# Gated one-hot rows made on VectorE per token, instead of compared on VectorE and gated on ScalarE

## The reference, cut to what matters

```python
def peer_ffn(h, w_query, sub_keys, expert_u, expert_v):
    ...
    cand_i = (si[:, :, 0, :, None] * N_KEYS + si[:, :, 1, None, :]).reshape(t, PEER_HEADS, PEER_TOPK * PEER_TOPK)
    top_s, pos = lax.top_k(cand_s, PEER_TOPK)
    idx = jnp.take_along_axis(cand_i, pos, axis=-1)
    gate = jax.nn.softmax(top_s, axis=-1).astype(h.dtype)
    ...
    def one_block(args):
        xi, ii, gi = args
        u = jnp.take(expert_u, ii, axis=0)
        a = jnp.einsum('ted,td->te', u, xi)
        w = gi * jax.nn.gelu(a, approximate=False)
        vv = jnp.take(expert_v, ii, axis=0)
        return jnp.einsum('te,ted->td', w, vv)
```

## Time and profile before

| | us |
|---|---|
| median of 3 runs | 1815.28 |
| lowest, highest | 1812.93, 1815.53 |
| profiled execution | 1814.15 |
| its span | 1812.4 |
| TensorE busy in the span | 1620.0 |
| VectorE busy | 1259.2 |
| ScalarE busy | 664.0 |
| GpSimd busy | 390.6 |

### The profile page before, as it was taken

How to read it: one execution, slowest core, us unless ns; L and a number is a source line. 1 busy time by engine, 2 the same in 40 slices (tenths; PEclk the granted TensorE clock), 3 DMA queues, 4 the chain that set the end, 5 groups by cost and what they waited for, 6 DMA issues and landing times.

```text
span 1812.4 us, 23042 instructions
## 1 busy us (share of the span) xinstructions
PE 1620.0 (89%) x7605; PEld 1306.1 (72%) x7605; DVE 1259.2 (69%) x2268; ACT 664.0 (37%) x1227; POOL 390.6 (22%) x326
## 2 busy tenths in 40 slices
PE   1999988999889999999999999688888888989996
PEld 0454565545489889989999999666666676768784
DVE  6457255339977889988888888666666666766556
ACT  2111133212378269438633333132323222323333
POOL 1103200000010003002366666422222222220000
PEclk9889999999989999999999999889999899999998
DMA  9853500000266459647999999988889787887663
GB/s 357 291 187 141 209 1 1 0 0 20 74 204 227 146 178 324 242 150 264 326 412 413 413 413 412 396 281 275 282 294 327 260 268 276 305 281 237 196 213 111
DMA packets 172763, 426.15 MB, mean 235 GB/s; under 512 B 13068, under 2 KB 62220, under 8 KB 169496
## 3 DMA queue, kind: packets, MB, share of 16 engines
q1 hardware_dynamic: 135808, 291.06, 45.3%
q0 software_dynamic: 36864, 134.23, 20.5%
q10 hardware_dynamic: 24, 0.02, 0.0%
HBM read 372.84 MB, written 52.43 MB: 235 GB/s over the span
## 4 chain that ended last, share of the span: by engine, by line
PE 55%; DVE 18%; DMA 13%; SPq 5%; issue 4%; ACT 4%; POOL 1%; DVEq 0%; ACTq 0%; POOLq 0%
PE bank L1153 7%; DMA shared<-gelu_dense 7%; PE bank L1154 7%; PE bank L1157 7%; PE bank L1097 5%; SPq L479 5%; PE bank L1099 5%; PE bank L1098 5%; PE bank L951 5%; PE bank L1026 3%; PE bank L961 3%; PE bank L1112 3%; DMA hT<-in_expert_u,idx_slot 2%; ACT weights L794 2%; DVE u_lo L1486 2%
## 5 line engine op out<-in xcount | busy, mean ns | idle before, releaser
L1153 PE MATMUL bank<-v_hi,w_hi 128*128 128x512 f32 x768 | 310.2, 404 | 81.9 <-DVE w_lo L1587 81.7
L1097 PE MATMUL bank<-h_hi,u_hi 128*128 128x384 f32 x1024 | 348.9, 341 | 23.0 <-DVE u_lo L1486 23.0
L1098 PE MATMUL bank<-h_lo,u_hi 128*128 128x384 f32 x1024 | 345.0, 337 | 0.0
L1099 PE MATMUL bank<-h_hi,u_lo 128*128 128x384 f32 x1024 | 345.0, 337 | 0.0
L1154 PE MATMUL bank<-v_lo,w_hi 128*128 128x512 f32 x768 | 306.6, 399 | 0.0
L867 ACT ACTIVATE v_hi<-weights 128x1024 fp32r<-128x1024 f32 x128 | 135.5, 1059 | 302.7 <-PE bank L1157 249.0
L1157 PE MATMUL bank<-v_hi,w_lo 128*128 128x512 f32 x768 | 242.0, 397 | 0.0
L1153 PEld LDWEIGHTS bank<-v_hi,w_hi 128*128 128x128 f32 x768 | 149.3, 194 | 123.3 <-DVE v_lo L1583 70.0
L1097 PEld LDWEIGHTS bank<-h_hi,u_hi 128*128 128x128 f32 x1024 | 194.4, 190 | 27.3 <-DVE u_lo L1486 16.6
L1583 DVE TENSOR_TENSOR v_lo<-weights,v_hi 128x1024 fp32r<-128x1024 f32 x128 | 156.5, 1222 | 77.3 <-ACT v_hi L867 75.0
L1486 DVE TENSOR_TENSOR u_lo<-weights,u_hi 128x1024 fp32r<-128x1024 f32 x128 | 156.0, 1223 | 66.8 <-PE bank L1099 65.7
(11 more groups left out here) (233 smaller groups left out, 2195.9 us busy)
## 6 DMA issues: line engine op xcount, KB each, us to landing
weights<-in_uT SPq DMA_DIRECT2D x128, 512.0 KB
weights<-in_expert_v SPq DMA_DIRECT2D x128, 512.0 KB, 4.8
weights<-in_w_ada SPq DMA_DIRECT2D x12, 2048.0 KB, 9.6
gates_dense<-weights SPq DMA_DIRECT2D x24, 1024.0 KB, 6.4
shared<-gelu_dense SPq DMA_DIRECT2D x64, 384.0 KB
weights<-gates_dense SPq DMA_DIRECT2D x16, 1536.0 KB, 13.4
gelu_dense<-weights SPq DMA_DIRECT2D x32, 384.0 KB
gelu_dense<-final_row SPq DMA_DIRECT2D x32, 384.0 KB
```

Source lines behind the costliest of these rows:

```text
L1097: nc.tensor.matmul(a, uh[:, k, :], h2_hi[:, :, k, :], start=(k == 0), stop=False)
L1098: nc.tensor.matmul(a, uh[:, k, :], h2_lo[:, :, k, :], start=False, stop=False)
L1099: ins = nc.tensor.matmul(a, ul[:, k, :], h2_hi[:, :, k, :], start=False, stop=(k == KC - 1))
L1153: nc.tensor.matmul(acc, wh, v_hi[:, r % 2, cols], start=begin, stop=False)
```

## The change

hot_i is made with its gate in one step on VectorE: for each of the 8 tokens of a half one instruction over 128 columns compares the row 0..127 with the token's key i and multiplies by the token's gate, key and gate both being per partition scalars. hot_j is made as before. ScalarE's gate_rows is gone with its semaphore hot_gated; what waited for it waits for hot_made.

```diff
-            def gate_rows(half):
-                act.wait_ge(hot_made, half + 1)
-                for q in range(HTOK):
-                    token = half % (P // HTOK) * HTOK + q
-                    rows = hot_i[:, half % HALVES, q, :]
-                    ins = nc.scalar.activation(rows, rows, ACT.Copy, scale=turned[:, half * HTOK // P % 2, 2, token:token + 1])
-                ins.then_inc(hot_gated, 1)
-
...
                 if d >= 2:
-                    act.wait_ge(hot_gated, (d - 1) * P // HTOK)
+                    act.wait_ge(hot_made, (d - 1) * P // HTOK)
...
-                gate_rows(d * P // HTOK)
                 product(m)
                 m += 1
-                gate_rows(d * P // HTOK + 1)
...
-                    if c < CHUNKS - 1:
-                        gate_rows(2 * g + 2)
-                        gate_rows(2 * g + 3)
...
             def build(half):
-                pe.wait_ge(hot_gated, half + 1)
+                pe.wait_ge(hot_made, half + 1)
...
                 at = half % (P // HTOK) * HTOK
-                for which, rows in ((1, hot_j), (0, hot_i)):
-                    key = turned[:, half * HTOK // P % 2, which, at:at + HTOK]
-                    ins = tt(rows[:, half % HALVES], iota128.unsqueeze(1).broadcast_to([P, HTOK, P]),
-                             key.unsqueeze(2).broadcast_to([P, HTOK, P]), ALU.is_equal)
+                picked = turned[:, half * HTOK // P % 2]
+                tt(hot_j[:, half % HALVES], iota128.unsqueeze(1).broadcast_to([P, HTOK, P]),
+                   picked[:, 1, at:at + HTOK].unsqueeze(2).broadcast_to([P, HTOK, P]), ALU.is_equal)
+                for q in range(HTOK):
+                    ins = ts(hot_i[:, half % HALVES, q, :], iota128, picked[:, 0, at + q:at + q + 1], picked[:, 2, at + q:at + q + 1],
+                             ALU.is_equal, ALU.mult)
                 ins.then_inc(hot_made, 1)
```

More of the change, by code:

```diff
@@ L331, in program @@
         gates_ready, iota_made = sem("gates_ready"), sem("iota_made")
-        hot_made, hot_gated, built = sem("hot_made"), sem("hot_gated"), sem("built")
+        hot_made, built = sem("hot_made"), sem("built")
         build_read = sem("build_read")
```

## The result

The changed kernel took **1824.42 us** in the median (1822.64 to 1826.73, eight runs), where the kernel before took 1815.4 beside it (1811.03 to 1821.07, eight runs). The ratio is 1.0048 [1.0031, 1.0066], or +8.8 us [5.6, 12.0]: slower by half a per cent, clear of the noise, inside the forecast range and 2.6 us under the forecast of 1827. The profiled execution took 1824.94 with a span of 1823.2. That is 10.8 more than before, of which the rows cannot give all to the change, as the last part of the account says.

The account below looks back on a forecast made before the run. TensorE's 7.95 us chunk was the floor, VectorE close behind at 7.97 and becoming the bound of d = 1 and 2. 9.4 + 2.5 = +11.9 us, from 1815.28 to 1827; range 1811 to 1845.

Parts of the forecast that it names:

- Step 1: Gatings removed from ScalarE, builds wait for VectorE directly; whole gain bounded by TensorE's idle time, 2 × 5.3 = 10.6 us.
- Step 2: hot_j's table kept on VectorE: comparisons of 1024 columns follow every 1.137 us, 0.070 of it for each instruction.
- Step 3: Eight 128-column instructions added per half on VectorE: p = 0.247 us each, double column rate and two scalar fetches paid.
- Step 4: VectorE's chunk becomes 9.65 us, passing TensorE's 7.95 and bounding d = 1 and 2: +4.7 per stage, +9.4 for two.
- my formula: VectorE's chunk 5.70 + 16p; stage change is 7 × (chunk − 7.95) − 1.9, against 5.3 us of lag before.
- my 0.20: Turning point between gain and loss at p = 0.20 us per new VectorE instruction; below it the change wins.
- Step 5: d = 0 has no dots: VectorE's chunk needs 7.4 us, under 7.95, so TensorE covers it: zero.
- Step 6: Ahead of the chunks a longer first half table delays u_lo by 0.83 us without slack: three stages, +2.5.
- Step 7: After the last chunk, 3.5 us of VectorE's lead over the next tile's selection is lost but covered: zero, 1.2 as bound.
- Step 8: No DMA or SP and GpSimd queue work moved; TensorE bounds after the last stage, so a shift is carried to the end.
- Rival D: GpSimd's gather issues hold up VectorE's new instructions in d = 1 and 2: 28 us more, 1855; chance 0.04 in full.
- The chances: Forecast case 0.46, A 0.12, B 0.19, C 0.12, D 0.04, near even 0.07; outcomes faster 0.23, within 0.17, slower 0.60.

Follow-up runs that it names:

- no scalar: Changed kernel with both per partition scalars of the hot_i instruction replaced by immediates (real keys and gates left out): 1800.68 us, ratio 0.9917 to the kernel before.
- one scalar: Changed kernel with the key as per partition scalar and an immediate in place of the gate: 1809.48 us, ratio 0.997 to the kernel before.
- half the columns: Changed kernel with hot_i's instructions over 64 of the 128 columns, the rest of the table left as it was: 1820.59 us, ratio 1.0021 to the kernel before.
- scalar-tensor-tensor: Changed kernel with hot_i made per token with the key as scalar and the gate as a broadcast tensor: 1831.73 us, ratio 1.0085 to the kernel before.
- mix of 2: In d = 1 and 2, two tokens per half by the new instruction, six compared together and gated by ScalarE; d = 0 as before: 1813.88 us, ratio 0.9989.
- mix of 2 in bf16: Two new, six compared tokens per half in all stages, compared in bf16 with tokens innermost, u_lo queued before the tables: 1809.59 us, ratio 0.9976 to the kernel before.
- uneven halves: The bf16 mix with first half 2 new and 6 compared tokens, second half 4 and 4, in all stages: 1803.97 us, ratio 0.994 to the kernel before.
- d = 0 alone: The change made in stage d = 0 only, d = 1 and 2 as in the kernel before: 1815.38 us, ratio 1.0.
- u_lo first: Changed kernel with u_lo queued ahead of the first two half tables: 1821.2 us, ratio 1.0047; again on another chip 1826.74, ratio 1.006, to the kernel before.
- second chip: Another chip, where the unaltered changed kernel was run again: 1828.82 us, ratio 1.0075 to the kernel before.
- d = 1 and 2 alone: The change made in stages d = 1 and 2 only, d = 0 as in the kernel before: 1823.89 us, ratio 1.0053.

## Why the prediction was right, step by step

One row holds all the kernels together: the stage of d = 1 and what it gives when it counts twice, for d = 1 and 2 (66.15 is the kernel before).

```
kernel               VectorE p   chunk   stage d=1   2 x (stage - 66.15)   measured [95%]
no scalar            0.134       7.98    59.45       -13.4                 -15.1 [-19, -11]
one scalar           0.196       8.88    64.58        -3.1                  -5.4 [-8.9, -2.0]
half the columns     0.224       9.26    67.34        +2.4                  +3.8 [-0.2, +8.0]
changed              0.257       9.81    71.10        +9.9                  +8.8 [+5.6, +12.0]
scalar-tensor-tensor 0.262       9.93    72.05       +11.8                 +15.4 [+11, +19]
mix of 2             -           8.71    65.50        -1.3                  -2.0 [-4.2, +0.2]
mix of 2 in bf16     -           8.51    64.13        -4.0                  -4.4 [-7.1, -1.6]
uneven halves        -           8.21    61.70        -8.9                 -10.9 [-15, -7]
```

Every measured interval holds the figure of its stages. What happens there is nearly the whole effect. (The chunk is the mean of seven, from u_lo to u_lo; in the kernel before it is 8.67, since the 8.77 of the earlier trace rows alternate as 7.97 and 9.58.)

- **Step 1, the whole gain is bounded by the idle time, 10.6: wrong in size.** With VectorE out of the way the stages fall from 66.15 to 59.45 and from 66.19 to 59.47, 6.7 us each, not 5.3, and the kernel without scalars gained 15. The 5.3 are what the rows leave idle; but the rows count more busy time for the same work while it has to wait. Here is the stage of d = 1, the kernel before and then the kernel without scalars:

```profile
667.65:733.80 66.15, 60.88 (x426) 58.40 (x426) 61.35 (x78) 59.66 (x162) 23.97 (x17) 1.00 0.87 308
```

```profile
664.98:724.44 59.46, 59.46 (x426) 58.61 (x426) 59.01 (x165) 26.57 (x47) 15.06 (x15) 1.00 0.92 332
```

  The same 426 matmuls are 60.88 us busy in one and 59.46 in the other: 5.3 of idle time and 1.4 of this make the 6.7.
- **Step 2** (70 ns for each instruction, 1.137 for 1024 columns): L1459 takes 1.13 to 1.14 from start to start.
- **Step 3, p = 0.247: right in each part.** 0.137 without scalars was 0.134; the double rate was 0.033 us for 64 columns; two scalars were 0.123 where I took 0.110. Together that is 0.010 more, and with it 0.16 us per chunk. The Trainium skill, VectorE: DVE Perf Modes, section "The perf-mode tier table", gives the double rate to tensor_scalar in fp32; the 0.033 us agree.
- **Step 4, +4.7 per stage: 4.95 and 4.90 measured, by errors that nearly cancel.** The chunk was 9.81, not 9.65. By my formula that is 7 × (9.81 − 7.95) − 1.9 − 5.3 = 5.8. Against the stage that TensorE alone sets, 59.45, the lags are 11.65 (changed), 12.6 (scalar-tensor-tensor), 7.9 (half the columns) and 5.1 (one scalar). 7 × (chunk − 7.95) less 1.4 gives 11.6, 12.5, 7.8 and 5.1. So the credit at the end of the stage is 1.4, a number fitted to these four kernels, and not 1.9, and what it is set against is the old lag of 6.7 and not the 5.3 of the idle rows. The longer chunk is worth +1.1, the smaller credit +0.5, the larger old lag −1.4. That is why the kernel with one scalar surprised me: it is 7 × 0.93 − 1.4 − 6.7 = −1.6 per stage, where −1.9 − 5.3 gave −0.7. The old lag of 6.7 is 7 × (8.67 − 7.95) = 5.0 from the chunks and 1.7 at the end of the stage, where the last two builds still wait 0.40 us for the gating and 0.86 for the copy. The stages alone part into gain and loss at a chunk of 7.95 + 8.1 / 7 = 9.11, p = 0.213, where my formula has 0.205; with the tables ahead, which my 0.20 counts, it is about 0.21.
- **Step 5, d = 0 covered: right.** TensorE is busy for all of it, the stage is 59.30 instead of 59.58, and the kernel with d = 0 alone came out at 1.0 [0.9985, 1.0014].
- **Step 6, +0.83 in each of three stages: right.** From the turned rows to the first chunk's u_lo it is 9.17 us in all three stages before (510.48 to 519.65 in the first) and 10.05, 10.07 and 10.07 after: +0.9. In d = 0 the shorter stage gives 0.3 back, and 0.6 stay. In d = 1 and 2 all of it stays. What my expectation for u_lo first had wrong is that another order of the queue gives it back: of the 0.9 it wins 0.4 there.
- **Step 7, a lead of 3.5 lost and covered: right, or too careful.** From the first chunk's u_lo to the last one's, seven chunks, d = 1 grows by 8.0 us (68.68 for 60.66). From there to the turned rows of d = 2 it was 86.67 before and is 83.66 after: 3.0 come back, since that u_lo was early before and is late now, and a last build ends 4.95 later, not 8.0. That makes the step's cost zero: from turn to turn it is 162.39 for 156.50, +5.9, which is the 0.9 ahead and the 4.95 of the stage. In the changed kernel on the second chip, and with d = 1 and 2 alone, it is 82.10 and +4.3, 1.6 in favour. This is the clock again. The rows behind the stage, up to the turned rows, of the changed kernel in its first profile and on the second chip:

```profile
738.00:819.00 81.00, 76.76 (x431) 75.65 (x430) 71.30 (x255) 27.38 (x37) 2.29 (x3) 0.98 0.53 183
...
778.60:782.00 3.40, 3.40 (x12) 3.40 (x12) 2.73 (x13) 0.00 (x0) 0.00 (x0) 0.50 0.81 275
```

```profile
736.00:817.00 81.00, 76.77 (x441) 75.65 (x440) 72.28 (x257) 28.50 (x40) 2.29 (x3) 1.00 0.54 185
```

  In the first the granted clock is 0.50 (1.2 GHz for 2.4) from 778.6 for 3.4 us, in which TensorE does 12 matmuls; in the 20 us before, at 1.00, it was busy for 17.44. In the second it stays at 1.00. All fourteen traces part this way: with such a stretch it is 81.3 to 81.5 us from the end of the stage to the turned rows, without one (five traces) 79.9 to 80.0. The five are all kernels in which VectorE is the bound, but three others of that kind have the stretch, so whether the change itself makes it rarer stays open.
- **Step 8, carried to the end: right.** From the rows it is −0.1 for d = 0, +4.3 to +5.9 for d = 1, 0.9 + 4.9 = +5.8 for d = 2: +10.0 to +11.6 us. With the same stretches of low clock on both sides it is +0.6, +5.9 and +5.8, which is 12.3, where the sum had 11.9. That d = 0 looks like zero and d = 1 sometimes like +4.3 goes with the clock, which the forecast did not look at. The medians say +8.8 [5.6, 12.0], and +13.6 [9, 18] on the second chip. The profiled pair's own +10.8 is no better witness: the turned rows of d = 0 come at 507.96 after and at 510.48 before, 2.5 us earlier with nothing changed ahead of them, and 1.7 us are added behind the stages.
- **Rival D did not occur in the changed kernel.** In d = 0 GpSimd issues nothing and eight new instructions take 2.13 us; beside the two gathers of each chunk they take 2.13. A small form of it shows in other kernels. Without scalars, the eight beside the gathers take 1.27 us and the next eight 1.16:

```profile
686.03 1.27 DVE L1462 TENSOR_SCALAR weights<-ada 128x128 f32<-128x128 f32 x8
```

```profile
686.09 0.98 POOL L611 DMA_INDIRECT hT<-in_expert_u,idx_slot  x1 [0.30 <-issue]
```

  One instruction is longer there, 0.25 us for 0.135, once per chunk, and it is the one during which the second gather's issue ends. With one scalar the first of the eight takes 0.04 longer, which is why that chunk is 8.88 and not 5.70 + 16 × 0.196 = 8.84. What lay behind the 0.68 of the earlier trace rows no run tested.
- **The chances.** Those of the cases add up to 0.62 for slower and 0.15 for within, where the prediction has 0.60 and 0.17; nothing hangs on it.

The right answer came by the right mechanism. The term that was most mis-sized is the room, 5.3 for 6.7. The errors of step 4 cancelled by luck, and near the turning point they would have mattered.

## What to carry to other kernels

Count per partition scalars as work: here each cost 0.061 us per instruction, nearly as much as the 128 columns themselves (0.067 at two columns a cycle), so taking a multiply off ScalarE and putting it on an engine that was already at the floor, by way of 8 small instructions, lost more than it saved. Before moving work, compare each engine's chunk with the floor of the stage (7.95 against 7.97 here), and take the room from a run with the suspect taken away, since idle time read from the rows was a fifth too small. When two engines are both near the floor, share the work so that the loop between them is shortest: what won was fewer and cheaper gatings in the loop, with a table that VectorE could still make in time. And before a microsecond in a trace is put down to a change, compare TensorE's granted clock over the same stretch.

## What the runs showed of the hardware

- **Scalars add up.** 128 columns of compare and multiply take 0.134, 0.196 and 0.257 us from start to start with none, one and two of them.
- **The new instructions make GpSimd's issue shorter.** The second gather of a chunk took 1.98 us before, when two comparisons of 1024 columns lay beside it. After it is

```profile
680.67 0.94 POOL L611 DMA_INDIRECT shared<-in_expert_u,idx_slot  x1 [0.30 <-issue]
```

  beside the tensor-scalars that begin at 680.61. It is 0.97 without scalars, 1.97 where d = 1 is as before, 1.71 in the first mix (768 columns of comparison) and 1.31 with the comparison in bf16. The Trainium skill, SBUF — State Buffer, section "Who interferes with whom", says that "A DVE instruction with two SBUF inputs contends with a GpSimd instruction that reads SBUF"; these rows agree. It also says that VectorE in a two-port mode and GpSimd block each other fully; with the new instructions, at two columns a cycle, no row shows either engine held for a whole instruction of the other. What shows is at most 0.12 us on one VectorE instruction per chunk. Issues are not on the path here, and no run isolated the cause.
- **A bf16 comparison with all operands adjacent** went at two columns a cycle: 0.47 us from start to start for 768 columns. ScalarE paid for the layout: from start to start a gating of 128 columns takes 0.36 us when it reads every sixth bf16 element and 0.31 when it reads every fourth (both in the kernel with uneven halves). Reading adjacent fp32 elements it was 0.29.
- **TensorE's clock moves the stretches between the stages.** One stretch of 3.4 us at a granted clock of 0.50 went with 1.6 and 1.4 us more from the end of the stage of d = 1 to the next turned rows, in two pairs of traces of one and the same kernel: 81.49 against 79.92 in the changed kernel, 81.34 against 79.90 with u_lo first.
